# Expert loop of a mixture-of-experts kernel: one wide up product, hidden transposes behind the rows', down passes by readiness

## The chip, the core and the metric

The kernel runs on one core of a Trainium2 chip. The core has a matrix engine (TensorE, PE in the rows; PEld is its loading of stationary operands), VectorE (DVE), ScalarE (ACT), GpSimd (POOL) and SyncE (SP, which here only issues transfers). The metric is the device time of one execution in microseconds; of several executions the median counts. A "profile" is one execution recorded by the hardware profiler.

## What is computed

One decoder layer on 1024 rows of 1024 numbers, float32: a mixer, a layer norm, then a mixture of 16 experts of which each row uses two, and a second layer norm. The part that matters here:

```python
def moe(x, router_w, router_b, w_gate, w_up, w_down):
    xt = x.reshape(B_ * S_, D_)                     # 1024 x 1024
    ...                                             # router: two experts and two weights for each row
    for e in range(N_EXPERTS):                      # 16
        hid = jax.nn.silu(xt @ w_gate[e]) * (xt @ w_up[e])      # 1024 -> 512
        out = out + combine[:, e:e + 1] * (hid @ w_down[e])     # 512 -> 1024
```

## The kernel before

The router sorts rows by expert into tiles of 128 rows that belong to one expert. An expert has one tile or more; the loop over experts is unrolled by registers that hold the number of extra tiles. Each tile runs the three products of one expert for 128 gathered rows and stores 128 rows of result. After the loop each row's two results are gathered, weighed, added to the residual and normalised.

**Precision.** Each float32 operand is split into a high part (rounded, made by ScalarE as a copy) and a low part (the rest, made by VectorE as a subtraction). A product is three passes, high x high, low x high and high x low (`PASSES`), summed in PSUM. So rows (`XR`), hidden values (`HR`) and weights (`wg`, `wu`, `wd`) all exist twice.

**Weights.** An expert's weights come as 12 units of 512 KB: units 0 to 3 gate, 4 to 7 up, 8 to 11 down. SP loads unit u of the next expert into its slot of `stage` once VectorE has subtracted unit u of the expert before (semaphore `expert_lo`, in code `xw_lo`). During the last tile of an expert ScalarE copies (`split_hi`, L654) and VectorE subtracts (`split_lo`, L804) the 12 units of the next one; ScalarE first waits until TensorE no longer needs the old unit (`xw_used`, or `gate_ps`, `up_ps`, `y_ps` for a product's last unit). In the other tiles this work is absent: `split(...)` does nothing there.

**One tile on TensorE** (`pe_experts`, `body`): gate product into bank 0 (L611, 8 k-steps x 3 passes, 512 columns); up product in two halves `a` of 256 columns, half 0 into bank 1 and half 1 into bank 7 (L622), with the transposes of the first hidden half in the middle of the second (`transpose_hidden(g, 0)`, L602); transposes of the next tile's gathered rows (`transpose_rows`, L595, 8); transposes of the second hidden half; down product (L636, 4 f-steps x 3 passes x 2 halves of 512 columns into banks 2 and 3), whose f-steps 0 and 2 wait for the low part of a hidden half (`hr_lo`).

**The other engines.** They run their own lists in program order and meet at semaphores. ScalarE: silu of gate (`sil_sb`), copies of hidden halves (`hidden_hi`, L670), copy of next rows (`rows_hi`, L662), copy of the down result (L691) and its store, with the unit copies strewn between. VectorE: hidden half = silu x up (`hidden`, L821), low part of hidden (`hidden_lo`, L825), low part of rows (`rows_lo`, L808), with the unit subtractions between. GpSimd gathers the next tile's rows (L544) once the transposes of the present ones are done. VectorE's list in a tile reads:

```python
hidden(g, 0); split(0); hidden_lo(g, 0)
hidden(g, 1); split(1); hidden_lo(g, 1)
split(2, 3); rows_lo(g + 1); split(4, 5, 6, 7, 8, 9, 10, 11)
```

## Time and profile before

| | |
|---|---|
| median of 3 runs | 1034.89 us (1032.19 to 1034.9) |
| span of the profiled execution | 1030.7 us |
| expert loop, first gate product to last down product | 514 to 949 us, 24 tiles |
| busy share of the span | TensorE 86%, VectorE 65%, ScalarE 44%, GpSimd 13% |
| granted TensorE clock, mean | 0.931 |

A profile page gives busy times and groups of instructions; the trace behind it can be asked for stretches of time, for groups by line and form, and for the instructions of an engine in order of time. In such rows a bracket like `[2.46 <-DVE split_rows L808]` says how long the engine had been idle and whose work released it. Matmuls are pipelined: the time of one row of n matmuls reaches past the start of the next row, so the start of the next row is what counts.

### The profile page before, as it was taken

The numbers are of one execution on the slowest core, as the hardware profiler recorded it, in microseconds if no ns is written. First come the engines' busy times: TensorE is split into PE (matmuls) and PEld (weight loads), VectorE is DVE, ScalarE is ACT, GpSimd is POOL, SyncE is SP. The second block draws the span as 40 slices with busy tenths as digits, with TensorE's granted clock in tenths as the row PEclk, the third lists the DMA queues.
The fourth block names the chain that finished last, engine by engine and source line by source line (L and its number), as shares of the span: only waits on it lengthen the run. The fifth ranks groups of instructions, "written<-read, shape, count | busy, mean of one in ns | idle before, by whom it ended". The sixth has DMA issues, their size and how long they took to land.

```text
span 1030.7 us, 15075 instructions
## 1 busy us (share of the span) xinstructions
PE 884.6 (86%) x4992; PEld 772.3 (75%) x4992; DVE 667.7 (65%) x981; ACT 455.7 (44%) x594; POOL 139.0 (13%) x168
## 2 busy tenths in 40 slices
PE   6999999999967999995199999999999999998000
PEld 6998887888755888884189898988989898897000
DVE  3441899983265778874837586676898662635695
ACT  3531110102355443313336686767888662645231
POOL 3000011011112112100100001000110100000583
PEclk9999999999996999996599999999999999999555
DMA  7620213314225433314657498695999863595671
GB/s 270 214 83 1 99 54 123 105 73 160 82 85 164 157 108 100 125 41 160 229 224 284 167 405 345 219 392 181 413 407 410 339 224 142 185 324 205 212 259 79
DMA packets 77509, 202.25 MB, mean 196 GB/s; under 512 B 7215, under 2 KB 27009, under 8 KB 77473
## 3 DMA queue, kind: packets, MB, share of 16 engines
q1 hardware_dynamic: 63984, 155.31, 41.8%
q0 software_dynamic: 9888, 33.76, 9.1%
q10 hardware_dynamic: 3600, 12.72, 3.1%
q8 instruction: 21, 0.34, 0.1%
q14 instruction: 16, 0.12, 0.0%
HBM read 167.14 MB, written 34.62 MB: 196 GB/s over the span
## 4 chain that ended last, share of the span: by engine, by line
PE 79%; DVE 9%; issue 7%; DMA 2%; ACT 1%; POOL 1%; DVEq 0%; SPq 0%; POOLq 0%; ACTq 0%
PE banks L1072 17%; PE banks L622 13%; PE banks L611 13%; PE banks L636 13%; PE banks L1069 8%; PE banks L1186 6%; PE banks L595 2%; DVE arena L849 2%; PE banks L1207 2%; PE banks L602 1%; PE banks L1053 1%; DMA arena<-in_x 1%; DVE split_weights L804 1%; PE banks L1121 1%; DVE small L865 1%
## 5 line engine op out<-in xcount | busy, mean ns | idle before, releaser
L804 DVE TENSOR_TENSOR split_weights<-arena,split_weights 128x1024 fp32r<-128x1024 f32 x192 | 223.7, 1218 | 1.0
L654 ACT ACTIVATE split_weights<-arena 128x1024 fp32r<-128x1024 f32 x192 | 190.7, 1052 | 12.2 <-ACT work L691 10.4
L1072 PE MATMUL banks<-split_weights 128*128 128x512 f32 (+2 forms) x960 | 182.5, 351 | 0.0
L1072 PEld LDWEIGHTS banks<-split_weights 128*128 128x128 f32 x960 | 156.2, 191 | 23.9 <-issue 1.4
L622 PE MATMUL banks<-split_weights,split_rows 128*128 128x256 f32 x1152 | 147.5, 284 | 0.0
L622 PEld LDWEIGHTS banks<-split_weights,split_rows 128*128 128x128 f32 x1152 | 142.7, 191 | 1.9
L611 PE MATMUL banks<-split_weights,split_rows 128*128 128x512 f32 x576 | 136.0, 392 | 2.5 <-DVE split_rows L808 2.5
L636 PE MATMUL banks<-split_weights,split_hidden 128*128 128x512 f32 x576 | 137.5, 394 | 0.0
L611 PEld LDWEIGHTS banks<-split_weights,split_rows 128*128 128x128 f32 x576 | 109.1, 190 | 25.6 <-issue 2.9
L636 PEld LDWEIGHTS banks<-split_weights,split_hidden 128*128 128x128 f32 x576 | 106.6, 188 | 21.6
L821 DVE TENSOR_TENSOR work<-work,banks 128x256 f32<-128x256 f32 x48 | 20.2, 421 | 116.0 <-PE banks L622 116.0
L1069 PE MATMUL banks<-split_weights 128*128 128x512 f32 x384 | 87.5, 390 | 0.0
L1270 ACT ACTIVATE split_weights<-arena 128x1024 fp32r<-128x1024 f32 (+2 forms) x28 | 25.6, 937 | 136.9 <-PE banks L1072 83.0
L1069 PEld LDWEIGHTS banks<-split_weights 128*128 128x128 f32 x384 | 71.9, 188 | 15.0
L1511 DVE SCALAR_TENSOR_TENSOR arena<-arena,small 128x1024 f32<-128x1024 f32 x60 | 74.2, 1277 | 0.4
L544 POOL DMA_INDIRECT work<-x_scratch,tile_tokens x25 | 24.5, 978 | 257.8 <-PE banks L595 257.2
L670 ACT ACTIVATE split_hidden<-banks 128x256 fp32r<-128x256 f32 x48 | 18.5, 385 | 76.9 <-PE banks L602 75.9
L1186 PE MATMUL banks<-split_weights,split_rows 128*128 128x512 f32 x192 | 49.6, 413 | 3.3 <-DVE split_rows L1714 3.3
L1580 DVE TENSOR_TENSOR work<-banks,work 128x512 f32<-128x512 f32 x24 | 16.5, 689 | 48.9 <-PE banks L1072 48.7
L1186 PE MATMUL banks<-split_weights 128*128 128x512 f32 x192 | 46.7, 396 | 0.0
L1186 PEld LDWEIGHTS banks<-split_weights,split_rows 128*128 128x128 f32 x192 | 37.1, 198 | 11.1 <-DVE split_rows L1714 3.5
L691 ACT ACTIVATE work<-banks 128x1024 f32<-128x1024 f32 x24 | 24.6, 1023 | 38.4 <-PE banks L636 38.4
(294 smaller groups left out, 991.2 us busy)
## 6 DMA issues: line engine op xcount, KB each, us to landing
arena<-in_w_gate SPq DMA_DIRECT2D x64, 512.0 KB, 6.2
arena<-in_w_up SPq DMA_DIRECT2D x64, 512.0 KB, 7.2
arena<-in_w_down SPq DMA_DIRECT2D x64, 512.0 KB, 7.9
y_scratch<-work ACTq DMA_DIRECT2D x24, 512.0 KB, 6.6
arena<-in_w_in SPq DMA_DIRECT2D x20, 512.0 KB, 5.5
arena<-in_x SPq DMA_DIRECT2D x16, 512.0 KB, 6.1
arena<-in_w_out SPq DMA_DIRECT2D x8, 512.0 KB, 5.1
x_scratch<-arena SPq DMA_DIRECT2D x8, 512.0 KB, 3.4
```

The costliest lines, as they stand in the source:

```text
L544: pool.indirect_dma_start(out=xe, out_offset=None, in_=x1_dram, in_offset=bass.IndirectOffsetOnAxis(ap=tok1, axis=0)).then_inc(xe_in, 16)
L611: last = pe.matmul(bank(0), XR[:, hx, k, :], wg[:, hw, k, :], start=(k == 0 and i == 0), stop=(k == KC - 1 and i == 2))
L622: last = pe.matmul(bank(up_bank[a])[:, 0:DH2], XR[:, hx, k, :], wu[:, hw, k, a * DH2:(a + 1) * DH2], start=(k == 0 and i == 0), stop=(k == ...
L636: last = pe.matmul(bank(2 + half), HR[:, hx, f, :], wd[:, hw, f, half * 512:half * 512 + 512], start=(f == 0 and i == 0), stop=(f == FC - ...
L654: act.activation(unit_split(u, 0), unit_slot(u), AF.Copy).then_inc(xw_hi, 1)
L691: act.activation(ys, psum[:, 2:4, :].rearrange("p a n -> p (a n)"), AF.Copy).then_inc(y_sb, 1)
L804: dve.tensor_tensor(unit_split(u, 1), unit_slot(u), unit_split(u, 0).bitcast(F32), ALU.subtract).then_inc(xw_lo, 1)
L1069: last = pe.matmul(b, wc[:, hw, k, f * P:(f + 1) * P], xT[:, hx, k, half * 512:half * 512 + 512], start=(k == 0 and i == 0), stop=(k == KC ...
L1072: last = pe.matmul(b[:, 0:width], xT[:, hx, k, j * P:(j + 1) * P], wc[:, hw, k, 0:width], start=(k == 0 and i == 0), stop=(k == KC - 1 and ...
L1186: last = pe.matmul(bank(6 + half), XRb[ch.b][:, hx, k, :], wo[:, hw, k, half * 512:half * 512 + 512], start=(k == 0 and i == 0), stop=(k = ...
L1270: act.activation(wc[:, 0, 2 * u:2 * u + 2, 0:width], staged_unit(n)[:, 0:2 * width].rearrange("p (k n) -> p k n", k=2), AF.Copy).then_inc( ...
L1511: last = dve.scalar_tensor_tensor(acc[:, f, :], cpad[:, f, i:i + SEQ], convw[:, f, i:i + 1], acc[:, f, :], ALU.mult, ALU.add)
```

## The change

It touches the expert loop alone. Up becomes one product of 512 columns into bank 1, with one signal in place of two (`up_ps` counts tiles). Both pairs of hidden transposes stand behind the transposes of the next rows, into banks 6 and 7. The down product no longer runs its three passes f by f: for each hidden half it waits for the high part, runs high x high and high x low for both f-steps, then waits for the low part and runs low x high. ScalarE's list moves unit 2 ahead of the hidden copies and unit 3 behind the rows' copy. VectorE's list puts units 0, 1 and 2 ahead of the hidden products and unit 3 behind the rows.

```diff
--- before.py
+++ after.py
@@ -420,7 +420,7 @@
             return 16 * (1 if n < 4 else n // 8 + (1 if n % 8 < 4 else 2))
 
 
-        up_bank, hidT_bank = (1, 7), (6, 0)
+        hidT_bank = (6, 7)
         WORD = T ** (NE // 2) - 1
         BEFORE = [staged_count(28 + (u - 4) % 8) // 16 for u in range(8)] + [1] * 4
 
@@ -442,7 +442,7 @@
         def wait_unit_used(eng, u, e, g):
 
             if u % 4 == 3:
-                eng.wait_ge((gate_ps, up_ps, y_ps)[u // 4], (2 * g + 2) if u // 4 == 1 else (g + 1))
+                eng.wait_ge((gate_ps, up_ps, y_ps)[u // 4], g + 1)
             else:
                 eng.wait_ge(xw_used, e * 9 + (u // 4) * 3 + u % 4 + 1)
 
@@ -612,31 +612,36 @@
                     if last_tile and k % 2 == 1 and k < KC - 1:
                         last.then_inc(xw_used, 1)
                 last.then_inc(gate_ps, 1)
-                for a in range(2):
-                    for k in range(KC):
-                        if a == 0 and k % 2 == 0:
-                            pe.wait_ge(xw_lo, e * UNITS + 4 + k // 2 + 1)
-                        if a == 1 and k == KC // 2:
-                            transpose_hidden(g, 0)
-                        for i, (hx, hw) in enumerate(PASSES):
-                            last = pe.matmul(bank(up_bank[a])[:, 0:DH2], XR[:, hx, k, :], wu[:, hw, k, a * DH2:(a + 1) * DH2],
-                                             start=(k == 0 and i == 0), stop=(k == KC - 1 and i == 2))
-                        if a == 1 and last_tile and k % 2 == 1 and k < KC - 1:
-                            last.then_inc(xw_used, 1)
-                    last.then_inc(up_ps, 1)
+                for k in range(KC):
+                    if k % 2 == 0:
+                        pe.wait_ge(xw_lo, e * UNITS + 4 + k // 2 + 1)
+                    for i, (hx, hw) in enumerate(PASSES):
+                        last = pe.matmul(bank(1), XR[:, hx, k, :], wu[:, hw, k, :], start=(k == 0 and i == 0), stop=(k == KC - 1 and i == 2))
+                    if last_tile and k % 2 == 1 and k < KC - 1:
+                        last.then_inc(xw_used, 1)
+                last.then_inc(up_ps, 1)
                 transpose_rows(g + 1)
+                transpose_hidden(g, 0)
                 transpose_hidden(g, 1)
                 pe.wait_ge(y_sb, PRIMED + g)
-                for f in range(FC):
-                    if f % 2 == 0:
-                        pe.wait_ge(hr_lo, 2 * g + f // 2 + 1)
-                    pe.wait_ge(xw_lo, e * UNITS + 8 + f + 1)
-                    for i, (hx, hw) in enumerate(PASSES):
-                        for half in range(2):
-                            last = pe.matmul(bank(2 + half), HR[:, hx, f, :], wd[:, hw, f, half * 512:half * 512 + 512],
-                                             start=(f == 0 and i == 0), stop=(f == FC - 1 and i == 2))
-                    if last_tile and f < FC - 1:
-                        last.then_inc(xw_used, 1)
+
+                def down(f, hx, hw):
+                    for half in range(2):
+                        last = pe.matmul(bank(2 + half), HR[:, hx, f, :], wd[:, hw, f, half * 512:half * 512 + 512],
+                                         start=(f == 0 and hx == 0 and hw == 0), stop=(f == FC - 1 and hx == 1))
+                    return last
+
+                for a in range(2):
+                    pe.wait_ge(hr_hi, 2 * g + a + 1)
+                    for f in (2 * a, 2 * a + 1):
+                        pe.wait_ge(xw_lo, e * UNITS + 8 + f + 1)
+                        down(f, 0, 0)
+                        down(f, 0, 1)
+                    pe.wait_ge(hr_lo, 2 * g + a + 1)
+                    for f in (2 * a, 2 * a + 1):
+                        last = down(f, 1, 0)
+                        if last_tile and f < FC - 1:
+                            last.then_inc(xw_used, 1)
                 last.then_inc(y_ps, 1)
 
             transpose_rows(0)
@@ -678,14 +683,12 @@
 
                 act.wait_ge(gate_ps, g + 1)
                 act.activation(sil, bank(0), AF.Silu).then_inc(sil_sb, 1)
-                split(0, 1)
+                split(0, 1, 2)
+                act.wait_ge(up_ps, g + 1)
                 hidden_hi(g, 0)
-                split(2)
                 hidden_hi(g, 1)
-                split(3)
-                act.wait_ge(up_ps, 2 * g + 2)
                 rows_hi(g + 1)
-                split(4, 5, 6, 7)
+                split(3, 4, 5, 6, 7)
                 act.wait_ge(y_ps, g + 1)
                 act.wait_ge(y_out, PRIMED + g * 16)
                 act.activation(ys, psum[:, 2:4, :].rearrange("p a n -> p (a n)"), AF.Copy).then_inc(y_sb, 1)
@@ -816,9 +819,9 @@
 
             def hidden(g, a):
                 half = slice(a * DH2, (a + 1) * DH2)
-                dve.wait_ge(up_ps, 2 * g + a + 1)
+                dve.wait_ge(up_ps, g + 1)
                 dve.wait_ge(sil_sb, g + 1)
-                dve.tensor_tensor(hid[:, half], sil[:, half], bank(up_bank[a])[:, 0:DH2], ALU.mult).then_inc(hid_sb, 1)
+                dve.tensor_tensor(hid[:, half], sil[:, half], bank(1)[:, half], ALU.mult).then_inc(hid_sb, 1)
 
             def hidden_lo(g, a):
                 dve.wait_ge(hr_hi, 2 * g + a + 1)
@@ -831,15 +834,13 @@
                         for u in units:
                             split_lo(e + 1, u)
 
+                split(0, 1, 2)
                 hidden(g, 0)
-                split(0)
+                hidden(g, 1)
                 hidden_lo(g, 0)
-                hidden(g, 1)
-                split(1)
                 hidden_lo(g, 1)
-                split(2, 3)
                 rows_lo(g + 1)
-                split(4, 5, 6, 7, 8, 9, 10, 11)
+                split(3, 4, 5, 6, 7, 8, 9, 10, 11)
 
             each_tile(dve, "dve", body, own)
```

On TensorE, from the end of up to the start of down in a tile; `work` holds the gathered rows and the hidden values, `hidden_ready` is `hid_sb`. Before:

```order
L622 MATMUL banks<-split_weights,split_rows 128x256 x17
L600 ISA
L602 MATMUL banks<-ident,work 128x128 [waits hidden_ready]
L602 MATMUL banks<-ident,work 128x128
L622 MATMUL banks<-split_weights,split_rows 128x256 x12
L593 ISA
L595 MATMUL banks<-ident,work 128x128 [waits rows_gathered]
L595 MATMUL banks<-ident,work 128x128 x7
L600 REGISTER_ALU
L602 MATMUL banks<-ident,work 128x128 [waits hidden_ready]
L602 MATMUL banks<-ident,work 128x128
L633 REGISTER_ALU [waits hidden_lo,down_copied]
```

And now:

```order
L619 MATMUL banks<-split_weights,split_rows 128x512 x5
L593 ISA
L595 MATMUL banks<-ident,work 128x128 [waits rows_gathered]
L595 MATMUL banks<-ident,work 128x128 x7
L600 ISA
L602 MATMUL banks<-ident,work 128x128 [waits hidden_ready]
L602 MATMUL banks<-ident,work 128x128
L600 REGISTER_ALU
L602 MATMUL banks<-ident,work 128x128 [waits hidden_ready]
L602 MATMUL banks<-ident,work 128x128
L637 REGISTER_ALU [waits hidden_hi,down_copied]
L630 MATMUL banks<-split_weights,split_hidden 128x512 [waits expert_lo]
```

Both pairs of hidden transposes now stand after the eight row transposes, and the wait ahead of down names `hidden_hi`, ScalarE's copy, where it named `hidden_lo`.

On VectorE, from the start of its list in a tile with unit work; L804 (now L807) subtracts a weight unit, L821 (L824) makes a hidden half. Before:

```order
L820 REGISTER_ALU [waits up_ready]
L821 TENSOR_TENSOR work<-work,banks 128x256 [waits silu_ready]
L803 ISA
L804 TENSOR_TENSOR split_weights<-arena,split_weights 128x1024 [waits expert_hi]
L825 TENSOR_TENSOR split_hidden<-banks,split_hidden 128x256 [waits hidden_hi]
L819 REGISTER_ALU
L821 TENSOR_TENSOR work<-work,banks 128x256 [waits silu_ready,up_ready]
L803 REGISTER_ALU
L804 TENSOR_TENSOR split_weights<-arena,split_weights 128x1024 [waits expert_hi]
L825 TENSOR_TENSOR split_hidden<-banks,split_hidden 128x256 [waits hidden_hi]
L803 REGISTER_ALU
L804 TENSOR_TENSOR split_weights<-arena,split_weights 128x1024 [waits expert_hi]
```

And now:

```order
L807 TENSOR_TENSOR split_weights<-arena,split_weights 128x1024 [waits expert_hi]
L806 REGISTER_ALU
L807 TENSOR_TENSOR split_weights<-arena,split_weights 128x1024 [waits expert_hi]
L806 REGISTER_ALU
L807 TENSOR_TENSOR split_weights<-arena,split_weights 128x1024 [waits expert_hi]
L822 REGISTER_ALU
L824 TENSOR_TENSOR work<-work,banks 128x256 [waits silu_ready,up_ready] x2
L827 ISA
L828 TENSOR_TENSOR split_hidden<-banks,split_hidden 128x256 [waits hidden_hi]
L827 REGISTER_ALU
L828 TENSOR_TENSOR split_hidden<-banks,split_hidden 128x256 [waits hidden_hi]
```

Three unit subtractions, each with its wait for ScalarE's copy (`expert_hi`), now stand ahead of both hidden products; one stood between them, the others behind.

## Rows read from the trace of the kernel before

**Rows 1.** Stretches: busy time of each engine, clock and DMA share of each.

```profile
core 0: us, PE busy (x) PEld busy (x) DVE busy (x) ACT busy (x) POOL busy (x), PEclk, DMA share, GB/s
...
60.00:500.00 440.00, 395.44 (x1974) 330.70 (x1972) 295.52 (x547) 126.46 (x204) 43.65 (x54) 0.95 0.32 108
...
760.00:940.00 180.00, 180.00 (x1079) 160.89 (x1078) 110.22 (x122) 111.17 (x130) 15.88 (x19) 1.00 0.72 268
```

**Rows 2.** Groups by form: busy us, mean ns of one, idle before them.

```profile
L654 ACT ACTIVATE split_weights<-arena 128x1024 fp32r<-128x1024 f32 x192 | 190.7, 1052 | 12.2 <-ACT work L691 10.4 <-DMA arena<-in_w_up 1.8
...
L622 PE MATMUL banks<-split_weights,split_rows 128*128 128x256 f32 x1152 | 147.5, 284 | 0.0
...
L611 PE MATMUL banks<-split_weights,split_rows 128*128 128x512 f32 x576 | 136.0, 392 | 2.5 <-DVE split_rows L808 2.5
...
L611 PEld LDWEIGHTS banks<-split_weights,split_rows 128*128 128x128 f32 x576 | 109.1, 190 | 25.6 <-issue 2.9
```

**Rows 3.** Order of time on TensorE, one tile: start us, us, engine, line.

```profile
786.32 5.60 PE L611 MATMUL banks<-split_weights,split_rows 128*128 128x512 f32 x24
791.76 4.48 PE L622 MATMUL banks<-split_weights,split_rows 128*128 128x256 f32 x36
796.07 0.41 PE L602 MATMUL banks<-ident,work 128*128 128x128 f32 x2
796.24 1.67 PE L622 MATMUL banks<-split_weights,split_rows 128*128 128x256 f32 x12
797.74 1.06 PE L595 MATMUL banks<-ident,work 128*128 128x128 f32 x8
798.64 0.40 PE L602 MATMUL banks<-ident,work 128*128 128x128 f32 x2
798.79 5.73 PE L636 MATMUL banks<-split_weights,split_hidden 128*128 128x512 f32 x24
804.36 5.60 PE L611 MATMUL banks<-split_weights,split_rows 128*128 128x512 f32 x24
```

**Rows 4.** Order of time on TensorE: the first gate product and a later one.

```profile
514.13 7.19 PE L611 MATMUL banks<-split_weights,split_rows 128*128 128x512 f32 x24 [2.46 <-DVE split_rows L808]
...
569.84 5.60 PE L611 MATMUL banks<-split_weights,split_rows 128*128 128x512 f32 x24
```

**Rows 5.** Order of time on ScalarE beside the tile of rows 3.

```profile
786.96 1.02 ACT L691 ACTIVATE work<-banks 128x1024 f32<-128x1024 f32 x1
...
788.67 3.91 ACT L654 ACTIVATE split_weights<-arena 128x1024 fp32r<-128x1024 f32 x4 [0.70 <-ACT work L691]
...
793.89 0.60 ACT L680 ACTIVATE work<-banks 128x512 f32<-128x512 f32 x1
794.38 2.00 ACT L654 ACTIVATE split_weights<-arena 128x1024 fp32r<-128x1024 f32 x2
796.52 0.39 ACT L670 ACTIVATE split_hidden<-banks 128x256 fp32r<-128x256 f32 x1
...
799.07 0.39 ACT L670 ACTIVATE split_hidden<-banks 128x256 fp32r<-128x256 f32 x1 [1.23 <-PE banks L602]
...
800.30 1.02 ACT L662 ACTIVATE split_rows<-banks 128x1024 fp32r<-128x1024 f32 x1
```

**Rows 6.** Order of time on ScalarE in three earlier tiles.

```profile
570.12 1.03 ACT L691 ACTIVATE work<-banks 128x1024 f32<-128x1024 f32 x1 [4.27 <-PE banks L636]
...
575.48 0.60 ACT L680 ACTIVATE work<-banks 128x512 f32<-128x512 f32 x1 [2.22 <-PE banks L611]
...
595.45 0.60 ACT L680 ACTIVATE work<-banks 128x512 f32<-128x512 f32 x1
```

**Rows 7.** Order of time on VectorE: ahead of the loop, and beside rows 3.

```profile
512.78 1.22 DVE L808 TENSOR_TENSOR split_rows<-banks,split_rows 128x1024 fp32r<-128x1024 f32 x1
...
785.19 9.20 DVE L804 TENSOR_TENSOR split_weights<-arena,split_weights 128x1024 fp32r<-128x1024 f32 x8
...
797.94 0.42 DVE L821 TENSOR_TENSOR work<-work,banks 128x256 f32<-128x256 f32 x1 [0.58 <-PE banks L622]
```

## Prediction

> **What bounds the kernel now.** I read four views, in this order. First the stretches: from 760 to 940 us TensorE is busy 180.00 of 180.00 us at a granted clock of 1.00, while VectorE is busy 110.22 us and ScalarE 111.17 us [rows 1]. So inside the expert loop the other engines cost nothing as long as they stay behind TensorE, and every 0.1 us of TensorE time per tile is on the path. Second the groups by form: they give the counts and the cost of a matmul [rows 2]. Third TensorE's order of time for one tile [rows 3]: its groups follow one another without one bracket of idle. Fourth ScalarE and VectorE beside it [rows 5 to 7], because the change makes TensorE wait for these two where it did not wait before.
>
> I put the zero of a tile's clock at the start of its gate product. In [rows 3] that is 786.32: gate 0 to 5.44, up 5.44 to 11.42 (with the first pair of hidden transposes inside it), row transposes from 11.42, second pair from 12.32, down from 12.47, next gate at 804.36 - 786.32 = 18.04. The down product thus takes 5.57.
>
> The gate product runs 576 matmuls [rows 2], 24 for each tile, so there are 24 tiles. The ScalarE copies of weight units are 192 [rows 2]: 12 stand ahead of the loop, and 15 tiles carry 12 each (split tiles; the other 9 I call plain). What matters below is how many split tiles stand right behind another split tile: their silu starts with no idle before it and is followed by split copies. There are 8 such, the first silu at 595.45 [rows 6], the last at 793.89 [rows 5].
>
> **Part 1: the up product at 512 columns.** Removed: 48 matmuls of 256 columns and the transposes between them, 5.98 us. Added: 24 matmuls of 512 columns. The gate product is the same form with the same moving and stationary tiles: 24 in 5.44 us, (5.60 - 0.39)/23 = 0.227 us apart [rows 3, 2]. The 36 narrow ones took 796.07 - 791.76 = 4.31 us, 0.120 us apart, so the wide form gains about 0.3 us of work, 0.07 us lies in the second piece (12 in 1.50 us), and 0.17 us are the two transposes, which only move. Up now ends, for the next instruction, at 10.88 instead of 11.42: -0.54 us. The Trainium skill, page "TensorE: Matmul & The Clock Gate", section "Back-to-back issue gap", speaks against this part: it gives columns/2.4 GHz plus 2.5 ns for a warm matmul, so an estimate by it has halving the count save 24 x 2.5 ns = 0.06 us a tile, and the whole would come out some 24 x 0.25 = 6 us later than my sum. The distances of [rows 3] show about 13 ns on top of the columns at both widths, so the trace decides against it.
>
> **Part 2: both pairs of hidden transposes behind the row transposes.** Rows start at 10.88 and take 0.90 us as now; the first pair can start at 11.78. It needs VectorE's first product. The last up matmul ends 0.16 us after the next group starts, at 11.04; VectorE starts 0.03 us after such an end (797.91 to 797.94) [rows 3, 7], takes 0.42 us and ends at 11.49. A released TensorE starts 0.13 us after VectorE's end (512.78 + 1.22 = 514.00, then 514.13) [rows 7, 4]: 11.62, before 11.78. So in a plain tile the row transposes hide the product. The first pair costs 0.15 us more on TensorE here, as the second pair does now.
>
> **Part 3: the wait ahead of the down product.** Before, the down product's first half was transposed, copied and subtracted while up was still running, so nothing was waited for. Now TensorE's down matmuls are queued behind a wait for ScalarE's copy of transposes that have only just been made. First pair at 11.78; ScalarE's copy starts 0.43 us later (798.64 to 799.07 [rows 3, 5]), takes 0.39 us, and TensorE is released about 0.13 us later. I take the VectorE release for the ScalarE one, which no row of the loop shows; the bound below is 0, above 0.26. Down starts at 11.78 + 0.95 = 12.73. Without the wait it would start at 11.78 + 0.30, so 0.65 us are idle. The new order of passes puts 8 matmuls (about 1.86 us) ahead of the first use of the low part, which VectorE makes 0.45 us after the copy, so no second wait; nor for the second pair, whose copy ends by about 13.0 against a first use at 14.6. Down keeps 24 matmuls and as many weight loads: 5.57 us. Plain tile: 12.73 + 5.57 = **18.30, that is +0.26 us**. In one line: -0.54 (up) + 0.15 (pair moved) + 0.65 (wait).
>
> **Part 4: three subtractions ahead of the hidden product on VectorE.** In a split tile VectorE must first finish units 0, 1 and 2, each behind ScalarE's copy of that unit, and ScalarE starts those only after the silu. Behind a plain tile the silu starts when gate is done, at 575.48 - 569.84 = 5.64 [rows 6, 4]; copies from 6.13, 0.95 us apart; subtractions from about 7.2, 1.14 us apart ((9.20 - 1.22)/7 [rows 7]), the third over at about 10.7, before up ends. No cost: 18.30.
> Behind a split tile ScalarE is late. The down copy starts 0.28 us after the down product is over (569.84 to 570.12 [rows 4, 6]), at 0.28 of the next tile (now 0.64: 786.96; the new order leaves ScalarE free by then). From there the distances of [rows 5] hold: 1.71 us to the four down copies, 5.22 us from these to the silu (a table load lies between), 0.49 us to the first split copy: 0.28 + 1.71 + 5.22 + 0.49 = 7.70. It takes 1.05 us, so VectorE's three start at 8.79, 9.93, 11.07, and VectorE is free for the hidden product at about **12.21** instead of 11.07. TensorE then gets its first pair at 12.21 + 0.42 + 0.13 = 12.76 instead of 11.78, down starts at 13.71, and the tile ends at 19.28: **+1.24 us**. Behind the late product queue the hidden copies, the rows' copy and split 3 to 7 on ScalarE. They end at 12.76 + 0.43 + 0.6 + 0.9 + 5 x 0.95 = 19.4 against a down copy asked for at 19.56, so the delay does not grow from tile to tile. VectorE's rest (rows, nine units) ends near 7.6 of the next tile, before 8.79.
>
> **What costs nothing.** SP issues a unit's load when VectorE has subtracted it, in the same order of units as before; the slot is asked for again one period later less the copy and the subtraction, and the period grows, so no load gets less time. ScalarE waited for loads 1.8 us in the whole run [rows 2]. If that cover were gone, each late load would add to ScalarE's chain. POOL's gather hangs on the row transposes, a whole tile ahead, and TensorE shows no idle at 797.74 [rows 3]; it moves with them. The extra wait for up on ScalarE ahead of its hidden copy is met long before the transposes. The unit-used signals of the down passes come later, but ScalarE reaches those units only after the down copy. The next gate product's low rows are subtracted about 4 us after VectorE starts the hidden product, 3 us ahead of need.
>
> **The sum.** 16 tiles x 0.26 + 8 tiles x 1.24 = 4.2 + 9.9 = 14.1 us. The profiled execution's span is 1030.7 us, so it becomes 1044.8; the median of the runs lies 4.2 us above that span, so 1034.89 + 14.1 = 1049.0 us. What comes after the loop starts when the last tile's result is stored and shifts whole.
>
> **Rivals.**
> A, VectorE is not late: the three subtractions are done before up ends in all split tiles. It needs ScalarE's silu 1.1 us earlier than its row at 793.89 less 786.32 = 7.57 [rows 5]; nothing else in the rows does that. Then 24 x 0.26 = 6.2: **1041.1**.
> B, waits cost more than 0.13 us to leave, 0.26 us: once per tile, twice in the eight: 32 x 0.13 = 4.2 more: **1053**.
> C, no change: the wide stream is bound by its weight loads alone. The gate's loads show 109.1/576 = 0.189 us each [rows 2]; at that distance up would take 4.55 us, 0.89 us less, in the 16 tiles that VectorE does not hold: 14.2 us, **1034.8**. It decides from a distance of 0.208 us downwards (0.45 us a tile, half the way, leaves 1042). Against it stands the same form in the gate product at 0.227. The same section of the Trainium skill gives about 131 ns for a sustained 512-column matmul beside its load; an estimate by that has up at 3.1 us and the kernel faster. The trace does not agree: 0.227.
> D, the clock: with TensorE idle up to 1.6 us in a tile, the granted clock may dip between 2.4 and 1.2 GHz. In the stretch from 60 to 500 us, idle 44.6 of 440 us, it was 0.95 on the mean [rows 1]. At 0.95 the 17.65 us of work a tile costs 0.93 more, 22 us in all: **1071**. The Trainium skill, same page, section "A second HAM failure mode: psum-queue depth-cycling", says that short idles between matmul groups can make the clock oscillate, which is this rival's mechanism. Here idle would be 2 to 8% of the loop, less than in that stretch, and most of its gaps are longer than these.
>
> **How the numbers follow.** The forecast case 0.72 (its own range 1046 to 1051), A 0.10, B 0.08, C 0.06, D 0.04. The range 1040 to 1054 takes in A and B and leaves 0.10 out; without A it would leave 0.20 out with no room for the bounds of part 3. About 0.3% (3 us) is what a measurement of this kernel can tell from no change: faster by more 0.02 and same 0.06 come from C and the low edge of A, slower 0.92 from the rest.
>
> **What the new profile would show.** Up: 24 matmuls of 512 columns in 5.44 us. Before down, idle of about 0.65 us with ScalarE's hidden copy as releaser, in all 24 tiles. In eight tiles, idle of about 1 us ahead of the first hidden pair, released by VectorE. Periods of 18.3 and 19.3 us and a clock of 1.00. The sum is wrong if those eight read 18.3 (A), if up takes under 5.2 us (C), or if the clock falls (D).

## The result, and the profile after

| | before | changed |
|---|---|---|
| median, device us | 1033.54 (1031.11 to 1034.9) | 1047.49 (1047.24 to 1047.89) |
| ratio | | 1.014, 95% interval 1.0123 to 1.0157 |
| span of the profiled execution | 1030.7 | 1045.7 |
| first gate product to last down product (starts) | 514.13 to 943.11: 428.98 | 513.20 to 958.79: 445.59 |

The changed kernel is slower by 1.4%. The forecast was 1049.0 us. The kernel before was timed again beside the experiments, 12 to 17 times each, with medians of 1031.1 to 1032.2 us; against those the growth is 15 to 16 us and not 14, and the loop itself, in the profiles, grew by 16.6. Two executions among the experiments, of 1228.79 and 1844.93 us, were in a slower state and are left out of the medians below. The page of the changed kernel first: fewer instructions on TensorE, which is yet busy for a smaller share. VectorE's unit subtractions (L807), which had waited 1.0 us in all, now wait 93.7 us for ScalarE's copies; that alone costs nothing, but it shows which queue the hidden products stand behind.

```profile
span 1045.7 us, 13947 instructions
...
PE 889.8 (85%) x4416; PEld 749.2 (72%) x4416; DVE 668.1 (64%) x981; ACT 455.1 (44%) x594; POOL 133.1 (13%) x168
...
L807 DVE TENSOR_TENSOR split_weights<-arena,split_weights 128x1024 fp32r<-128x1024 f32 x192 | 222.1, 1220 | 93.7 <-ACT split_weights L659 93.6
...
L630 PE MATMUL banks<-split_weights,split_hidden 128*128 128x512 f32 x576 | 137.4, 394 | 9.1 <-ACT split_hidden L675 8.8
...
L619 PE MATMUL banks<-split_weights,split_rows 128*128 128x512 f32 x576 | 134.7, 389 | 0.0
```

TensorE in order of time, changed kernel: one late tile (a split tile behind a split tile), from the gate product at 797.93, and the plain tile behind it, from 817.34. They answer to [rows 3].

```profile
797.93 5.60 PE L611 MATMUL banks<-split_weights,split_rows 128*128 128x512 f32 x24
803.37 5.61 PE L619 MATMUL banks<-split_weights,split_rows 128*128 128x512 f32 x24
808.81 1.05 PE L595 MATMUL banks<-ident,work 128*128 128x128 f32 x8
810.61 0.83 PE L602 MATMUL banks<-ident,work 128*128 128x128 f32 x4 [0.75 <-DVE work L824]
811.77 5.73 PE L630 MATMUL banks<-split_weights,split_hidden 128*128 128x512 f32 x24 [0.32 <-ACT split_hidden L675]
817.34 5.60 PE L611 MATMUL banks<-split_weights,split_rows 128*128 128x512 f32 x24
822.78 5.61 PE L619 MATMUL banks<-split_weights,split_rows 128*128 128x512 f32 x24
828.23 1.05 PE L595 MATMUL banks<-ident,work 128*128 128x128 f32 x8
829.12 0.64 PE L602 MATMUL banks<-ident,work 128*128 128x128 f32 x4
830.17 5.73 PE L630 MATMUL banks<-split_weights,split_hidden 128*128 128x512 f32 x24 [0.41 <-ACT split_hidden L675]
835.73 5.60 PE L611 MATMUL banks<-split_weights,split_rows 128*128 128x512 f32 x24
```

Gate start to gate start is 19.41 us in the late tile and 18.39 in the plain one (before: 18.04 in both). There are eight late tiles, and but for the loop's first tile no others of that length; a first silu at 595 and a last at 794 had marked them in the trace of before. Up takes 5.44 us (822.78 to 828.23), as the gate product does.

The bracket of 0.41 us ahead of down understates the loss. It counts from the modelled end of the transposes, 829.76; by starts, the four transposes would let down begin 0.30 us after 829.12, and it begins 1.05 us after. For a pipelined engine the distance of starts is the cost.

Beside the late tile, VectorE and then ScalarE of the changed kernel:

```profile
806.73 3.50 DVE L807 TENSOR_TENSOR split_weights<-arena,split_weights 128x1024 fp32r<-128x1024 f32 x3 [1.07 <-ACT split_weights L659]
810.14 0.75 DVE L824 TENSOR_TENSOR work<-work,banks 128x256 f32<-128x256 f32 x2
```

```profile
805.15 0.60 ACT L685 ACTIVATE work<-banks 128x512 f32<-128x512 f32 x1
805.64 2.95 ACT L659 ACTIVATE split_weights<-arena 128x1024 fp32r<-128x1024 f32 x3
811.15 0.72 ACT L675 ACTIVATE split_hidden<-banks 128x256 fp32r<-128x256 f32 x2 [2.56 <-PE banks L602]
...
829.55 0.66 ACT L675 ACTIVATE split_hidden<-banks 128x256 fp32r<-128x256 f32 x2 [4.39 <-PE banks L602]
```

VectorE begins its three subtractions at 806.73, behind ScalarE's copy that ends at about 806.7, and its hidden products at 810.14, 12.21 us into the tile, while up ended at 808.97. TensorE's first hidden transpose waits for it.

### The profile page after: what moved, and what is told of

Its sections match the earlier page's. It is cut to its first block, busy times and chain, and to the rows that moved or that the text cites. A ratio compares the mean times of both kernels' runs of the same rounds, so it can differ in the third digit from the quotient of the medians.

```text
span 1045.7 us, 13947 instructions
## 1 busy us (share of the span) xinstructions
PE 889.8 (85%) x4416; PEld 749.2 (72%) x4416; DVE 668.1 (64%) x981; ACT 455.1 (44%) x594; POOL 133.1 (13%) x168
## 4 chain that ended last, share of the span: by engine, by line
PE 70%; issue 10%; DVE 8%; ACT 7%; DMA 1%; ACTq 1%; POOL 1%; SPq 0%; POOLq 0%; DVEq 0%
PE banks L1073 17%; PE banks L630 10%; PE banks L611 9%; PE banks L1070 8%; PE banks L619 8%; PE banks L1187 8%; ACT split_weights L659 4%; DVE arena L850 2%; PE banks L1208 1%; PE banks L595 1%; DVE split_weights L807 1%; PE banks L602 1%; ACT work L694 1%; PE banks L1054 1%; ACT split_hidden L675 1%
## 5 line engine op out<-in xcount | busy, mean ns | idle before, releaser
L807 DVE TENSOR_TENSOR split_weights<-arena,split_weights 128x1024 fp32r<-128x1024 f32 x192 | 222.1, 1220 | 93.7 <-ACT split_weights L659 93.6
L659 ACT ACTIVATE split_weights<-arena 128x1024 fp32r<-128x1024 f32 x192 | 187.6, 1055 | 11.4 <-PE banks L611 6.3
L611 PE MATMUL banks<-split_weights,split_rows 128*128 128x512 f32 x576 | 136.2, 392 | 2.5 <-DVE split_rows L811 2.5
L619 PE MATMUL banks<-split_weights,split_rows 128*128 128x512 f32 x576 | 134.7, 389 | 0.0
L611 PEld LDWEIGHTS banks<-split_weights,split_rows 128*128 128x128 f32 x576 | 109.2, 190 | 25.7 <-issue 2.9
L619 PEld LDWEIGHTS banks<-split_weights,split_rows 128*128 128x128 f32 x576 | 108.1, 188 | 22.4
L675 ACT ACTIVATE split_hidden<-banks 128x256 fp32r<-128x256 f32 x48 | 16.3, 382 | 86.5 <-PE banks L602 86.5
L1187 PE MATMUL banks<-split_weights,split_rows 128*128 128x512 f32 x192 | 49.9, 414 | 2.5 <-DVE split_rows L1715 2.5
L824 DVE TENSOR_TENSOR work<-work,banks 128x256 f32<-128x256 f32 x48 | 18.0, 418 | 46.7 <-PE banks L619 46.7
L1187 PEld LDWEIGHTS banks<-split_weights,split_rows 128*128 128x128 f32 x192 | 37.4, 200 | 10.4 <-DVE split_rows L1715 2.7
## 6 DMA issues: line engine op xcount, KB each, us to landing
arena<-in_w_gate SPq DMA_DIRECT2D x64, 512.0 KB, 5.8
arena<-in_w_up SPq DMA_DIRECT2D x64, 512.0 KB, 7.5
arena<-in_w_down SPq DMA_DIRECT2D x64, 512.0 KB, 7.4
y_scratch<-work ACTq DMA_DIRECT2D x24, 512.0 KB, 8.0
arena<-in_w_in SPq DMA_DIRECT2D x20, 512.0 KB, 5.2
arena<-in_x SPq DMA_DIRECT2D x16, 512.0 KB, 6.5
arena<-in_w_out SPq DMA_DIRECT2D x8, 512.0 KB, 5.2
x_scratch<-arena SPq DMA_DIRECT2D x8, 512.0 KB, 4.4
```

Of the source, the lines that this page charges most:

```text
L611: last = pe.matmul(bank(0), XR[:, hx, k, :], wg[:, hw, k, :], start=(k == 0 and i == 0), stop=(k == KC - 1 and i == 2))
L619: last = pe.matmul(bank(1), XR[:, hx, k, :], wu[:, hw, k, :], start=(k == 0 and i == 0), stop=(k == KC - 1 and i == 2))
L659: act.activation(unit_split(u, 0), unit_slot(u), AF.Copy).then_inc(xw_hi, 1)
L675: act.activation(HR[:, 0, 2 * a:2 * a + 2], bank(hidT_bank[a])[:, 0:DH2].rearrange("p (f n) -> p f n", f=2), AF.Copy).then_inc(hr_hi, 1)
L807: dve.tensor_tensor(unit_split(u, 1), unit_slot(u), unit_split(u, 0).bitcast(F32), ALU.subtract).then_inc(xw_lo, 1)
L1187: last = pe.matmul(bank(6 + half), XRb[ch.b][:, hx, k, :], wo[:, hw, k, half * 512:half * 512 + 512], start=(k == 0 and i == 0), stop=(k = ...
```

## The experiments

Each group of experiments has its own runs of the kernel before, and its median moved between 1031.1 and 1033.5 us, so a difference of medians between groups is uncertain by some 2 us; a ratio is always to the kernel before. The profiled loops begin anywhere from 512.0 to 516.1 us, whatever is changed in the loop, and a part of the first tile runs below full clock; that is noise of some 2 us, and the tile's length, which repeats to 0.04 us within a kernel behind the first tile, is the sharper measure. Lengths below are gate start to gate start.

**One subtraction behind the hidden work.** VectorE's list in the changed kernel:

```diff
-split(0, 1, 2)
+split(0, 1)
 hidden(g, 0); hidden(g, 1); hidden_lo(g, 0); hidden_lo(g, 1)
+split(2)
 rows_lo(g + 1)
```

> The changed kernel, with one thing moved: on VectorE the subtraction of unit 2 stands behind the hidden work (units 0 and 1 stay ahead of it). Theory (VectorE reaches the hidden product 1.14 us late in the eight split tiles behind split tiles, because three subtractions stand ahead of it): VectorE is free at 11.07 us of the tile instead of 12.21, just when up ends, so those eight tiles fall from 19.41 to about 18.39 us, 8 x 1.02 = 8.2 us in all: about 1039.3 us. TensorE's idle ahead of the first hidden pair (0.75 us each) is gone, the one ahead of down stays. Rival (these tiles are longer for another reason: transfers, or ScalarE's own chain): they stay at 19.4 and the time within 2 us of 1047.5.

Measured: 1038.27 us, ratio 1.0063 (1.004 to 1.0086). All tiles but the first are 18.41 or 18.42 us long, the late ones gone. TensorE and VectorE of this kernel in a tile that had been late:

```profile
800.95 1.05 PE L595 MATMUL banks<-ident,work 128*128 128x128 f32 x8
801.84 0.64 PE L602 MATMUL banks<-ident,work 128*128 128x128 f32 x4
802.89 5.75 PE L630 MATMUL banks<-split_weights,split_hidden 128*128 128x512 f32 x24 [0.41 <-ACT split_hidden L675]
```

```profile
798.86 2.36 DVE L807 TENSOR_TENSOR split_weights<-arena,split_weights 128x1024 fp32r<-128x1024 f32 x2 [1.07 <-ACT split_weights L659]
801.15 0.75 DVE L824 TENSOR_TENSOR work<-work,banks 128x256 f32<-128x256 f32 x2
```

The transposes follow the rows' again without a bracket, and the product starts right at up's end. So one subtraction of 1.14 us, at the head of a queue, was worth 8 us of the kernel by tile lengths (9.2 by the medians). The rival falls.

**Down passes in the old order, in the changed kernel.**

```diff
-for a in range(2):
-    pe.wait_ge(hr_hi, 2 * g + a + 1)
...
+for f in range(FC):
+    if f % 2 == 0:
+        pe.wait_ge(hr_lo, 2 * g + f // 2 + 1)
```

> The changed kernel, with the down product's passes back in the old order: f by f, each hidden half waiting for its low part before the first matmul. Theory (down's start hangs on the chain behind the hidden transposes): the chain grows by VectorE's subtraction, which ends at 830.39 against ScalarE's end at about 829.93; with releases of 0.09 us from VectorE and 0.24 us from ScalarE that is +0.31 us in each of 24 tiles, 7.4 us: about 1055 us. Rival (the order of passes is worth nothing, because the second half's wait comes last anyway): within 2 us of 1047.5.

Measured: 1064.07 us, ratio 1.0317 (1.0293 to 1.0341), more than the 1055 expected. Plain tiles are 18.87 us, +0.48 and not +0.31: VectorE's subtraction ends at 842.68 and down starts at 842.92, so its release costs 0.24 us here too, as ScalarE's does. Late tiles are 19.88 us (+0.47), but three of the eight are 21.5, because there the down product itself takes 7.35 us for its 24 matmuls where it takes 5.73 elsewhere. TensorE in one of them, VectorE in a plain tile, then the stretches around 802 us (columns as in [rows 1]):

```profile
800.95 0.83 PE L602 MATMUL banks<-ident,work 128*128 128x128 f32 x4 [0.75 <-DVE work L817]
802.57 7.35 PE L634 MATMUL banks<-split_weights,split_hidden 128*128 128x512 f32 x24 [0.79 <-issue]
...
842.92 5.74 PE L634 MATMUL banks<-split_weights,split_hidden 128*128 128x512 f32 x24 [0.88 <-DVE split_hidden L821]
```

```profile
842.26 0.76 DVE L821 TENSOR_TENSOR split_hidden<-banks,split_hidden 128x256 fp32r<-128x256 f32 x2 [0.79 <-ACT split_hidden L668]
```

```profile
780.00:800.00 20.00, 18.48 (x88) 15.24 (x86) 16.57 (x18) 16.02 (x18) 1.32 (x2) 1.00 1.00 372
800.00:805.00 5.00, 3.46 (x13) 2.61 (x13) 3.83 (x7) 3.50 (x6) 0.97 (x1) 0.82 1.03 418
805.00:810.00 5.00, 5.00 (x20) 3.99 (x20) 5.00 (x5) 2.85 (x4) 0.41 (x1) 0.84 0.98 356
```

The granted clock is 1.00 up to 800 us and 0.82 to 0.84 in the ten behind it, so between its two levels of 2.4 and 1.2 GHz it stood at the lower one for a part of that time: in smaller steps the same view shows 1.00 up to 803 us, 0.50 from 804 to 806 and 1.00 again from 808. This follows two idles of 0.75 and 0.79 us, between 800.20 and 802.57 us. The five other late tiles have the same two idles and keep their clock. (The 0.88 us in the fence is the single idle of a plain tile.) 24 x 0.48 us and 3 x 1.6 us make 16.3 us; the medians of the two kernels differ by 16.6, the ratios by 18 us. What follows: in this arrangement the new order of passes earns its keep.

**Up in two halves again, in the changed kernel.** Both pairs of transposes stay behind the rows'.

```diff
+for a in range(2):
 for k in range(KC):
...
-    last = pe.matmul(bank(1), XR[:, hx, k, :], wu[:, hw, k, :], ...)
+    last = pe.matmul(bank(up_bank[a])[:, 0:DH2], XR[:, hx, k, :], wu[:, hw, k, a * DH2:(a + 1) * DH2], ...)
```

> The changed kernel, with the up product back in two halves of 256 columns in banks 1 and 7, but both pairs of hidden transposes still behind the row transposes. Theory (the wide form saves 0.31 us of TensorE per tile, 48 x 0.120 against 24 x 0.227): 16 tiles grow by 0.31 us, 5.0 us in all; the eight tiles that VectorE holds keep their length, since there TensorE waits anyway: about 1052.5 us. Rival (width is worth nothing): within 2 us of 1047.5. Rival (the early first half lets the hidden product of half 0 run ahead and shortens the wait before down): no gain expected from that either, since the row transposes hide the product already.

Measured: 1053.8 us, ratio 1.0217 (1.0191 to 1.0243). Plain tiles 18.73 us (+0.34), late ones 19.43 (+0.02). In the fence, TensorE of this kernel: the 48 narrow matmuls take 5.75 us from start to start, the 24 wide ones of the changed kernel 5.44.

```profile
807.30 5.92 PE L620 MATMUL banks<-split_weights,split_rows 128*128 128x256 f32 x48
813.05 1.06 PE L595 MATMUL banks<-ident,work 128*128 128x128 f32 x8
```

So the wide form is worth 0.31 us of TensorE a tile, and nothing where TensorE waits for VectorE. 16 x 0.34 is 5.4 us of the 6.3 by which the medians differ; in the profile another 1.3 us lie in the first tile, 21.73 us against 20.13, whose gate product ran longer at the loop's cold start (8.59 against 7.34 us). Read against the kernel before, this run prices the other half of the change: it differs from it by the place of the transposes, the order of passes and the two queues, without the wide product, and its plain tiles are 18.73 - 18.04 = 0.69 us longer.

**The order of passes alone, in the kernel before.**

```diff
-for f in range(FC):
-    if f % 2 == 0:
-        pe.wait_ge(hr_lo, 2 * g + f // 2 + 1)
...
+for a in range(2):
+    pe.wait_ge(hr_hi, 2 * g + a + 1)
```

> The kernel before, with only the new order of down passes (high part waited for first, low x high last in each half). Theory (nothing is waited for at down's start in the kernel before, so readiness has nothing to bring): within 1 us of the kernel before, 1033.5 us. Rival (four matmuls in a row on the same stationary tile run faster or slower than two): down product other than 5.57 us per tile; 0.1 us each would be 2.4 us in all.

Measured: 1032.39 us, ratio 1.0005 (0.9987 to 1.0023), all tiles but the first 18.04 us, the down product 5.57 us. The order is worth something only where down waits, and four matmuls in a row on one stationary tile run as two did.

**A kernel beside its expectation.** The next text describes moved waits; by mistake the kernel that ran had another edit on the first experiment's kernel, namely two of the eight row transposes moved behind the hidden ones. The moved waits ran later, under "The wait on the matmul".

```diff
-transpose_rows(g + 1)
+transpose_rows(g + 1, range(6))
 transpose_hidden(g, 0)
 transpose_hidden(g, 1)
+transpose_rows(g + 1, range(6, KC))
```

> The kernel of e1_units01, with TensorE's waits for the down result's copy and for the down weights moved ahead of the row transposes, so that ScalarE's high copy is the only wait left right ahead of down and sits on its first matmul. In the runs so far a wait that stands on a matmul was left 0.05 us after VectorE's end (the first hidden pair, late tiles), one that stands ahead of it on the sequencer 0.24 us after ScalarE's or VectorE's end. Theory (the place of the wait sets that difference): down starts 0.15 us sooner in 24 tiles, 3.6 us: about 1034.7 us against 1038.3. Rival (the difference is ScalarE's own release, or the cost of a cold start): within 1 us of e1_units01.

Measured, for the two transposes moved: 1039.1 us, ratio 1.0078 (1.0059 to 1.0098), tiles 18.30 us instead of 18.41. TensorE and ScalarE of it:

```profile
837.32 0.83 PE L596 MATMUL banks<-ident,work 128*128 128x128 f32 x6
837.99 0.83 PE L604 MATMUL banks<-ident,work 128*128 128x128 f32 x4
838.66 0.39 PE L596 MATMUL banks<-ident,work 128*128 128x128 f32 x2
839.15 3.02 PE L633 MATMUL banks<-split_weights,split_hidden 128*128 128x512 f32 x12
```

```profile
838.53 0.71 ACT L678 ACTIVATE split_hidden<-banks 128x256 fp32r<-128x256 f32 x2 [3.03 <-PE banks L604]
```

The first transpose starts 0.22 us sooner, but it now comes behind a wait and ScalarE starts 0.54 us after it instead of 0.43, so half the gain is lost. No bracket stands ahead of down, and still down starts only when the copy is done (838.53 + 0.38 = 838.91, then 839.15).

**One copy more, three copies more.** Ahead of ScalarE's first hidden copy, in the first experiment's kernel:

```diff
 act.wait_ge(hidT_ps, 2 * g + a + 1)
+if a == 0:
+    for i in range(n):          # n = 1, then 3
+        act.activation(scratch[:, i], bank(hidT_bank[a])[:, 0:DH2], AF.Copy)
```

> The kernel of e1_units01, with one more ScalarE copy of the first hidden half (256 columns, into a spare tile) ahead of the real one. Theory (down's start hangs on ScalarE's copy): the copies follow at 0.28 us, so each of 24 tiles grows by 0.28 us, 6.7 us: about 1045 us, at a granted clock of 1.00 in the loop. Rival (the idle ahead of down has another cause): no change.

> As e7_copy_twice, with three more copies. Theory: each tile grows by 3 x 0.28 = 0.84 us over e1_units01, 20.2 us: about 1058.5 us, if the granted clock holds. TensorE then sits idle 1.25 us in a row in every tile. In e2_old_passes the granted clock fell for some microseconds in three of the eight tiles that had two waits of 0.75 and 0.88 us close together, and down took 7.35 us there instead of 5.73. Rival (idle time itself makes the clock fall, from about 1.2 us on): some tiles grow by 1.6 us more, and the time lies above 1062 us.

Measured: 1045.96 us, ratio 1.0149 (1.0125 to 1.0174), tiles 18.67 us (+0.26); and 1059.84 us, ratio 1.0275 (1.0255 to 1.0295), tiles 19.23 us (+0.82), a granted clock of 1.00 from 530 to 940 us. The chain through ScalarE's copy is thus on the path in every tile, at nearly its full price: copies that follow one another at 0.28 us cost 0.26 to 0.27 us each. With three copies TensorE shows 1.24 us idle ahead of every down product and not one slow tile, so the rival of idle time as such falls; what made the clock fall in three tiles above, two idles within 2.4 us or something else, stays open. The two kernels also ran on different chips.

```profile
834.74 0.64 PE L603 MATMUL banks<-ident,work 128*128 128x128 f32 x4
836.63 5.73 PE L631 MATMUL banks<-split_weights,split_hidden 128*128 128x512 f32 x24 [1.24 <-ACT split_hidden L679]
```

**The wait on the matmul.** In the first experiment's kernel:

```diff
+pe.wait_ge(y_sb, PRIMED + g)
+pe.wait_ge(xw_lo, e * UNITS + UNITS)
 transpose_rows(g + 1)
 transpose_hidden(g, 0)
 transpose_hidden(g, 1)
-pe.wait_ge(y_sb, PRIMED + g)
...
-        pe.wait_ge(xw_lo, e * UNITS + 8 + f + 1)
```

> The kernel of e1_units01, with TensorE's waits for the down result's copy and for the down weights moved ahead of the row transposes, so that only ScalarE's high copy is left ahead of down, and its wait sits on the first matmul; the row transposes stay together. Theory (a wait on the sequencer is left 0.24 us after the release, one on a matmul about 0.05 to 0.1): tiles of about 18.25 us instead of 18.41, 3.6 us in all: about 1034.7 us against 1038.3. Rival (the 0.24 us are the same wherever the wait stands): tiles of 18.4 us, the time within 1 us of e1_units01.

Measured: 1036.56 us, ratio 1.0045 (1.0024 to 1.0065), all tiles 18.22 us, 0.19 less than 18.41. TensorE and ScalarE of it:

```profile
836.66 0.64 PE L602 MATMUL banks<-ident,work 128*128 128x128 f32 x4
837.53 4.83 PE L631 MATMUL banks<-split_weights,split_hidden 128*128 128x512 f32 x20 [0.23 <-ACT split_hidden L675]
```

```profile
837.10 0.66 ACT L675 ACTIVATE split_hidden<-banks 128x256 fp32r<-128x256 f32 x2 [3.13 <-PE banks L602]
```

The first copy ends at 837.10 + 0.38 = 837.48 and down starts at 837.53: 0.05 us instead of 0.24. The copy and the transposes are the same, and no wait but ScalarE's is left between the transposes and down. The edit also makes one wait of the four for down weights, which was not tested by itself; from its start, down takes 5.57 us here and 5.59 in the first experiment. By time alone this run does not separate from the first experiment (the intervals overlap), by tile length it does.

**The chain in four pieces.** Product, transpose, high copy and low part each in pieces of 128 columns, with three row transposes moved between the pairs and the waits as just shown:

```diff
-transpose_rows(g + 1); transpose_hidden(g, 0); transpose_hidden(g, 1)
+transpose_rows(g + 1, range(5)); transpose_hidden(g, 0); transpose_rows(g + 1, range(5, KC)); transpose_hidden(g, 1)
...
-dve.tensor_tensor(hid[:, half], sil[:, half], bank(1)[:, half], ALU.mult).then_inc(hid_sb, 1)
+for f in range(2):
+    part = slice(a * DH2 + f, (a + 1) * DH2, 2)
+    dve.tensor_tensor(hid[:, part], sil[:, part], bank(1)[:, part], ALU.mult).then_inc(hid_sb, 1)
```

> The kernel of e5_wait_last, with the chain behind up cut finer: hidden product, transpose, high copy and low part go in four pieces of 128 columns (transposes in banks 6, 7, 0, 1), and three of the eight row transposes stand between the first and the second pair. Theory (what is left of the loss is the chain up, product, transpose, copy, down, less the TensorE work that can lie beside it): first product 0.27 us, ready at 11.33 us of the tile; transpose at 11.44; ScalarE's copy from 11.79 to 12.06; down at about 12.3 instead of 12.83, just behind the last transposes. Tiles of 17.88 us instead of 18.41 (before: 18.04): 12.7 us off e1_units01, about 1026 to 1028 us, 4 us under the kernel before. Rival (small instructions cost their fixed part on VectorE and ScalarE, and the subtractions of units fall behind): no better than e5_wait_last, 1034 to 1037 us.

Measured: 1030.55 us, ratio 0.9991 (0.998 to 1.0002): no difference from the kernel before, and 2.5 us above the expected range. 16 tiles are 17.9 us as expected, the eight late ones 18.19. In the one from 787.40 VectorE starts the products at 798.79, 11.39 us into the tile: the tile is shorter, ScalarE's chain behind the tile before is not (VectorE gets its first unit 9.11 us into this tile, 8.80 into a late tile of the changed kernel), so even two subtractions are one too many. And the first two transposes take 0.41 us from start to start, where two take 0.15. VectorE in that late tile, then TensorE in a plain one:

```profile
796.51 2.36 DVE L810 TENSOR_TENSOR split_weights<-arena,split_weights 128x1024 fp32r<-128x1024 f32 x2 [1.07 <-ACT split_weights L661]
798.79 0.87 DVE L829 TENSOR_TENSOR work<-work,banks 128x128 f32<-128x128 f32 x4
```

```profile
816.47 0.72 PE L596 MATMUL banks<-ident,work 128*128 128x128 f32 x5
817.02 0.57 PE L604 MATMUL banks<-ident,work 128*128 128x128 f32 x2
817.43 0.50 PE L596 MATMUL banks<-ident,work 128*128 128x128 f32 x3
```

**Finer still.** Both points mended:

```diff
-transpose_hidden(g, 0); transpose_rows(g + 1, range(5, KC)); transpose_hidden(g, 1)
+transpose_hidden(g, 0, (0,)); transpose_rows(g + 1, (5,)); transpose_hidden(g, 0, (1,)); transpose_rows(g + 1, (6, 7)); transpose_hidden(g, 1)
-split(0, 1); hidden ...; split(2); rows_lo(g + 1)
+split(0); hidden ...; split(1, 2); rows_lo(g + 1)
```

> The kernel of e6_quarters, with two things moved. On VectorE only the subtraction of unit 0 stands ahead of the hidden products: the eight tiles that read 18.19 us should fall to the 17.91 of the others, 2.2 us. On TensorE the first two hidden transposes, which stood together and took 0.41 us where two take 0.15, have one row transpose between them, and the other two row transposes behind: about 0.1 to 0.2 us less idle in 24 tiles, tiles of 17.75 us, 2.4 to 4.8 us. Theory: 1024 to 1027 us, clear below the kernel before. Rival (down hangs on ScalarE's first copy and not on TensorE's list): tiles of 17.9 us, about 1028.5 us.

Measured: 1027.37 us, ratio 0.9954 (0.9937 to 0.9972): faster than the kernel before, by half a percent. All tiles but the first are 17.82 to 17.84 us, between the expected 17.75 and the rival's 17.9. TensorE is busy 400.00 of 400.00 us from 530 to 930, and its order of time has no bracket:

```profile
828.94 0.71 PE L596 MATMUL banks<-ident,work 128*128 128x128 f32 x5
829.49 0.38 PE L604 MATMUL banks<-ident,work 128*128 128x128 f32 x1
829.71 0.27 PE L596 MATMUL banks<-ident,work 128*128 128x128 f32 x1
829.82 0.28 PE L604 MATMUL banks<-ident,work 128*128 128x128 f32 x1
829.94 0.39 PE L596 MATMUL banks<-ident,work 128*128 128x128 f32 x2
830.16 0.41 PE L604 MATMUL banks<-ident,work 128*128 128x128 f32 x2
830.32 5.71 PE L635 MATMUL banks<-split_weights,split_hidden 128*128 128x512 f32 x24
```

The tile is 0.21 us shorter than the 18.04 us of before. The wide product and the moved pair had promised more, 0.54 - 0.15 = 0.39 us. The rest is in the transposes, in spite of a full busy share: the twelve take 830.32 - 828.94 = 1.38 us from start to start, where in one stream they take 0.89 + 0.30 = 1.19.

## Why the prediction was right

**What bounds the loop.** Right. TensorE was full before, every wait put in front of it was paid, and the two experiments with extra copies show it at 0.27 us for each copy.

**Part 1, up.** Up takes 5.44 us, as predicted; the narrow form in its place takes 0.31 us more. The wide matmuls stand 0.227 us apart, as in the gate product. So the trace's distances held against two figures of the Trainium skill, page "TensorE: Matmul & The Clock Gate", section "Back-to-back issue gap": the saving of 0.06 us, an estimate worked out from its 2.5 ns for each matmul, and its 131 ns for a sustained matmul of 512 columns.

**Part 2, the moved transposes.** Right to 0.01 us: first hidden transpose at 829.12 - 817.34 = 11.78 us in a plain tile, without a wait for VectorE.

**Part 3, the wait ahead of down.** The mechanism was right, one term was undersized: the release of TensorE took 0.24 us, not 0.13. The 0.13 came from one row at the loop's start [rows 7, 4]; 0.24 was inside the bound of 0.26 that was kept for the range. Start of transpose to ScalarE 0.43 us, copy 0.38, release 0.24, down 5.56: 11.78 + 6.61 = 18.39, against 18.30. This was rival B, for one of its two waits. One reading was off without harm: the second pair's copy is first used behind twelve down matmuls and not eight, at 12.73 + 12 x 0.232 = 15.5 us and not at 14.6.

**Part 4, VectorE's queue.** VectorE reached the hidden product at 12.21 us of the late tile, the very number predicted. There the first transpose followed VectorE's end by 0.05 us and not 0.13, ScalarE followed the transpose by 0.54 and not 0.43, and the release took 0.24: 19.41 against 19.28. Eight late tiles were counted and eight came.

**What was said to cost nothing.** ScalarE waited 0.9 us for loads in the whole run, 1.8 before; no tile behind the first but the eight grew beyond the common length.

**The sum.** 14.1 us were predicted. The loop, from first gate to last down, grew by 16.6 us: 8 x 1.37 + 14 x 0.355, and 0.7 in the first and the last tile. The work around it took 1.6 us less than in the profile of before, which nothing in the change explains and which is within the 2 us by which loop starts differ between profiles. The medians differ by 14.0 us. So the closeness of the total owes something to chance: each tile was undersized by about 0.1 us, and the surroundings, and a median of before that lay 1 to 2 us above the later ones, gave it back.

**The rivals.** A (VectorE not late) is excluded by the late tiles and by the first experiment, which made it come true. Its condition was misstated: VectorE at 11.07 instead of 12.21 asks for a silu 1.1 us before the predicted 0.28 + 1.71 + 5.22 = 7.21, so at 6.1 and not 1.1 us before 7.57. B came for the down wait only. C is excluded by up's 5.44 us. D did not come in the changed kernel, where the clock is 1.00 from 530 to 950 us, but a fall of the clock did come in the second experiment, in three tiles, with waits ahead of down 0.5 us longer; what decides it is open.

## What to carry to other kernels

When one engine is full, an edit that shortens its work but joins two steps that had overlapped must first be costed as a chain: end of the producer, each hop through the other engines with its release, less what the full engine can do meanwhile. Here 0.54 us of saved work bought a chain 0.75 us too long, and three steps together paid for it: the last wait on the matmul itself (18.41 to 18.22 us a tile), the chain in quarters with three row transposes between the pairs (to 17.90, not tested apart), and a finer order of the transposes (to 17.82). On the in-order queue of a helper engine, look at what stands ahead of the instruction that the full engine waits for, in its latest case: one unit of background work put ahead cost half of the whole loss (8 of 16.6 us). And let the last wait that can come late be the one that the waiting instruction itself carries.

## What the runs showed of the hardware beyond what was expected

- TensorE left a wait that sat on a sequencer instruction 0.24 us after the releasing engine's end, ScalarE's or VectorE's, and one that sat on the matmul or transpose itself 0.05 to 0.06 us after it. At the loop's start it was 0.13 us before and 0.14 in the changed kernel, which neither explains.
- ScalarE started 0.43 us after the first of a pair of transposes that followed other transposes without a gap, and 0.54 us after one that had been waited for. With a signal for each transpose, in the two kernels in quarters, it was 0.42.
- With waits of 0.75 and 0.79 us within 2.4 us the granted clock fell in three of eight tiles (down product 7.35 instead of 5.73 us); with one wait of 1.24 us ahead of every down product it was 1.00 from 530 to 940 us. Why is open.
